# A two-layer hybrid decoder step on one core: the first step behind a norm goes set by set over both weight halves, with smaller first and last sets, a split sum of squares, and an earlier weight split

## The reference, cut to what matters

```python
for layer in range(DEPTH):                      # 2 layers
    mp = adaln(c_prompt, w_ada[layer], b_ada[layer])   # 6 vectors: shift, scale, gate, twice
    ms = adaln(c_sample, w_ada[layer], b_ada[layer])
    hp = modulate(yp, g_mix[layer], mp[0], mp[1])      # rms_norm(x, g) * (1 + scale) + shift
    hs = modulate(ys, g_mix[layer], ms[0], ms[1])
    ...                                          # layer 0: hp @ w_in_ab, conv and GLA mixers
    ...                                          # layer 1: hp @ w_in_cd, gMLP and attention
    yp = yp + mp[2][:, None, :] * (op @ w_out[layer])
    ys = ys + ms[2][:, None, :] * (os_ @ w_out[layer])
    yp = swiglu_sublayer(yp, mp[3], mp[4], mp[5], g_ffn[layer], w_ffn_gate[layer], ...)
    ys = swiglu_sublayer(ys, ms[3], ms[4], ms[5], g_ffn[layer], w_ffn_gate[layer], ...)
y_prompt = rms_norm(yp, g_final)
y_sample = rms_norm(ys, g_final)
```

## Time and profile before

| what | value |
|---|---|
| median of 3 executions | 2903.96 us (2903.19 to 2906.10) |
| the profiled execution's own time | 2900.26 us |
| its span | 2898.3 us |
| mean granted TensorE clock | 0.957 of full speed |
| PE busy (matmuls) | 2741.6 us, 95% of the span |
| DVE, ACT, POOL busy | 48%, 40%, 3% |
| the chain that ended last | PE 87%, DVE 4%, DMA 4%, ACT 3%, the rest 2% |

### The profile page before, as it was taken

The page is one execution under the profiler, slowest core; times in us unless marked ns, Lnnn a source line. Parts: engine busy times, 40 slices in busy tenths (PEclk is TensorE's granted clock), DMA queues, the critical chain, the costliest instruction groups (busy, mean ns, idle before and its releaser), DMA issues.

```text
span 2898.3 us, 47711 instructions
## 1 busy us (share of the span) xinstructions
PE 2741.6 (95%) x20153; PEld 2520.2 (87%) x20153; DVE 1402.5 (48%) x1845; ACT 1149.1 (40%) x1429; POOL 87.8 (3%) x116
## 2 busy tenths in 40 slices
PE   5899997989999999999999899798999999999998
PEld 1698875878888888898999799688999999999998
DVE  1599856343444333344444556435545444454444
ACT  2333254343344322334343446424444423444443
POOL 1000010000000000000000000101000000000000
PEclk7899986999999999999999999779999999999999
DMA  9667783766777688777634433224344344444443
GB/s 386 273 253 291 277 200 97 292 233 262 281 276 276 262 317 329 282 277 287 233 141 167 163 139 144 73 93 170 120 170 168 132 160 178 174 163 155 147 160 132
DMA packets 75774, 603.57 MB, mean 208 GB/s; under 512 B 21029, under 2 KB 22373, under 8 KB 24050
## 3 DMA queue, kind: packets, MB, share of 16 engines
q1 hardware_dynamic: 75634, 601.54, 56.2%
HBM read 592.01 MB, written 9.49 MB: 208 GB/s over the span
## 4 chain that ended last, share of the span: by engine, by line
PE 87%; DVE 4%; DMA 4%; ACT 3%; issue 1%; SPq 0%; POOL 0%; DVEq 0%; POOLq 0%; ACTq 0%
PE ps L654 26%; PE ps L656 25%; PE ps L655 25%; PE ps L784 5%; DMA pre_ring<-in_w_ada 3%; DMA aring<-in_w_ada 1%; DVE w_lo L1437 1%; ACT w_hi L1087 1%; PE ps L797 0%; DVE cacc L1532 0%; DVE act_lo L1635 0%; PE ps L769 0%; ACT tn L1250 0%; DVE tn L1616 0%; PE ps L1017 0%
## 5 line engine op out<-in xcount | busy, mean ns | idle before, releaser
L1437 DVE TENSOR_TENSOR w_lo<-raw,w_hi 128x2048 fp32r<-128x2048 f32 (+1 forms) x402 | 835.7, 2080 | 1112.6 <-ACT w_hi L1087 1112.4
L654 PE MATMUL ps<-act_hi,w_hi 128*128 128x288 f32 x4320 | 1294.3, 300 | 43.3 <-DVE act_lo L1635 31.4
L655 PE MATMUL ps<-act_hi,w_lo 128*128 128x288 f32 x4320 | 1279.0, 296 | 0.0
L656 PE MATMUL ps<-act_lo,w_hi 128*128 128x288 f32 x4320 | 1274.3, 295 | 0.0
L1087 ACT ACTIVATE w_hi<-raw 128x2048 fp32r<-128x2048 f32 (+1 forms) x402 | 699.3, 1741 | 1086.3 <-PE ps L656 1074.9
L654 PEld LDWEIGHTS ps<-act_hi,w_hi 128*128 128x128 f32 x4320 | 814.0, 188 | 104.4 <-issue 94.9
L656 PEld LDWEIGHTS ps<-act_lo,w_hi 128*128 128x128 f32 x4320 | 817.4, 189 | 0.0
L655 PEld LDWEIGHTS ps<-act_hi,w_lo 128*128 128x128 f32 x4320 | 815.4, 189 | 0.1
L654 PE MATMUL ps<-hid_hi,w_hi 128*128 128x288 f32 x1408 | 420.6, 299 | 8.6 <-DVE w_lo L1437 8.6
L655 PE MATMUL ps<-hid_hi,w_lo 128*128 128x288 f32 x1408 | 417.0, 296 | 0.0
L656 PE MATMUL ps<-hid_lo,w_hi 128*128 128x288 f32 x1408 | 415.5, 295 | 0.0
(11 more groups left out here) (271 smaller groups left out, 1429.9 us busy)
## 6 DMA issues: line engine op xcount, KB each, us to landing
aring<-in_w_ada SPq DMA_DIRECT2D x176, 1024.0 KB, 8.0
raw<-in_w_gu SPq DMA_DIRECT2D x88, 2048.0 KB, 8.1
raw<-in_w_dn SPq DMA_DIRECT2D x64, 1408.0 KB, 6.0
raw<-in_w_ab SPq DMA_DIRECT2D x20, 2048.0 KB, 8.1
raw<-in_w_out SPq DMA_DIRECT2D x16, 2048.0 KB, 8.2
raw<-in_w_cd SPq DMA_DIRECT2D x13, 2048.0 KB, 8.1
pre_ring<-in_w_ada SPq DMA_DIRECT2D x16, 1024.0 KB, 10.2
aring<-in_state_glaT SPq DMA_DIRECT2D x4, 1024.0 KB, 7.4
```

The lines of the kernel that those rows point to most:

```text
L654: pe.matmul(bank, w_hi[:, h, cols], hi[:, kt, :], start=begin, stop=False)
L655: pe.matmul(bank, w_lo[:, h, cols], hi[:, kt, :], start=False, stop=False)
L656: mm = pe.matmul(bank, w_hi[:, h, cols], lo[:, kt, :], start=False, stop=end)
L1437: dve.tensor_tensor(w_lo[:, h, 0:w], raw[:, par, h * w:(h + 1) * w], w_hi[:, h, 0:w].bitcast(F32), ALU.subtract).then_inc(split_done, 1)
```

## The change

The change has five parts.

1. **Restart.** The first step behind norms 1, 2 and 3 is done by a new function `restart` on PE: for each set of tiles it does half 0 and then half 1 of that set, into two PSUM banks, before it waits for the next set. An ada pair of that step now stands ahead of it.
2. **Sets.** For these norms the 16 tiles go in five sets of 2, 4, 4, 4 and 2 tiles, where there were four sets of 4.
3. **The splits around it.** Ahead of the norm, half 1 of the first step is split in two parts of 8 tiles: ACT does the first part ahead of the epilogue's squares and the second behind them; DVE does both behind its residual. `scales` moves from the norm's start to the step before it. Behind the restart, half 0 of the following step is split as 6 and 10 tiles: the first part may start when PE is through with half 0 of the second set (`part_done`), the second when half 0 of the whole restart is done; PE waits for the second part only ahead of tile 6.
4. **The last square.** For norms 1 to 4 POOL adds only 15 squares; PE multiplies the last square with the ones itself and accumulates.
5. **Ahead of `down`.** `then_wait` is no longer set for a step that stands ahead of a `down` segment, so half 1 of the first `down` step is split ahead of the last `gu` epilogue. (The segment `gu` that begins layer 1's feed-forward has its first body outside the loop now, since its first step is a restart.)

```diff
-    _s.peel = _s.bodies - 1 if _s.unrolled else int(_s.bodies == 2 or _s.opens or _s.kind == "out")
+    _s.peel = _s.bodies - 1 if _s.unrolled else int(_s.bodies == 2 or _s.opens or _s.kind == "out" or
+                                                    _s.kind == "gu" and _s.first == 0)
...
-        _a.then_wait = not isinstance(_b, Seg) or "down" in (_a.kind, _b.kind)
+        _a.then_wait = not isinstance(_b, Seg) or _a.kind == "down"
...
+PE_SQUARES = [39, 55, 79, 95]
+SETS = [(0, 2), (2, 6), (6, 10), (10, 14), (14, 16)]
+EARLY = 6
...
-                for k in range(n):
+                for k in range(n - (q + n - 1 in PE_SQUARES)):
...
-                pe.wait_ge(split_done, n * 2 + (h + 1))
+                in_parts = h == 0 and isinstance(n, int) and n - 1 in RESTARTS
+                if in_parts:
+                    pe.wait_ge(part_split, RESTARTS.index(n - 1) + 1)
+                else:
+                    pe.wait_ge(split_done, n * 2 + (h + 1))
...
+                    if in_parts and k == EARLY:
+                        pe.wait_ge(split_done, n * 2 + 1)
...
+            def restart(n, par):
+
+                pe.wait_ge(drained, n - 1)
+                for k0, k1 in SETS:
+                    pe.wait_ge(act_ready, sets[0] * KT + k1)
+                    for h in range(2):
+                        bank = ps[:, 2 * par + h, 0:T]
+                        if k0 == 0:
+                            pe.wait_ge(split_done, n * 2 + (h + 1))
+                        for kt in range(k0, k1):
+                            cols = slice(kt * P, (kt + 1) * P)
+                            pe.matmul(bank, w_hi[:, h, cols], act_hi[:, kt, :], start=(kt == 0), stop=False)
+                            pe.matmul(bank, w_lo[:, h, cols], act_hi[:, kt, :], start=False, stop=False)
+                            mm = pe.matmul(bank, w_hi[:, h, cols], act_lo[:, kt, :], start=False, stop=(kt == KT - 1))
+                        if k1 == EARLY and h == 0:
+                            mm.then_inc(part_done, 1)
+                        if k1 == KT:
+                            mm.then_inc(half_done, 1)
...
-                pe.matmul(ps[:, STAT_BANK, 0:T], ones[:], ssq[:], start=True, stop=True).then_inc(stat_ready, 1)
+                mm = pe.matmul(ps[:, STAT_BANK, 0:T], ones[:], ssq[:], start=True, stop=not split)
+                if split:
+                    pe.wait_ge(sq_ready, last + 1)
+                    mm = pe.matmul(ps[:, STAT_BANK, 0:T], ones[:], square_of(last), start=False, stop=True)
+                mm.then_inc(stat_ready, 1)
...
+                    if first and n in RESTARTS:
+                        if p is not None:
+                            ada_pair(p)
+                        restart(n, par)
+                        continue
...
+            def split_behind_restart(seg, n, par):
+
+                act.wait_ge(part_done, RESTARTS.index(n - 1) + 1)
+                high_part(seg, n, par, 0, 0, EARLY).then_inc(part_hi, 1)
+                act.wait_ge(half_done, n * 2 - 1)
+                high_part(seg, n, par, 0, EARLY, KT).then_inc(hi_done, 1)
...
+                    if nxt and end and seg.norm_next:
+                        act.wait_ge(half_done, n * 2 + 2)
+                        high_part(nxt, n + 1, 1 - par, 1, 0, CT).then_inc(first_hi, 1)
                     epilogue(seg, n, par, ls)
...
+                    if nxt and end and seg.norm_next:
+                        high_part(nxt, n + 1, 1 - par, 1, CT, KT).then_inc(hi_done, 1)
+                    elif nxt and hurry and not seg.mixed_next:
                         split(nxt, n + 1, 1 - par, 1)
...
-                scales(k, 0, KT)
                 if norm_base(k):
                     dve.wait_ge(act_ready, norm_base(k))
                 dve.wait_ge(rstd_ready, NORM_STATS[k])
-                for g in range(4):
+                for g in range(len(SETS)):
                     scaled(k, g)
                     samples(k, g)
                     if g:
                         lo(k, g - 1)
-                lo(k, 3)
+                lo(k, len(SETS) - 1)
```

More of the change, by code:

```diff
@@ L144, with sets_of, set_no, taken_by_pe @@
 SQUARES = [0, 16, 24, 40, 56, 64, 80, 96]
+PE_SQUARES = [39, 55, 79, 95]
 NORM_STATS = [1, 3, 4, 6, 7]
+SETS = [(0, 2), (2, 6), (6, 10), (10, 14), (14, 16)]
+EARLY = 6
 Y_PARTS = [slice(0, 2), slice(2, 4), slice(4, 8), slice(8, 12), slice(12, 14), slice(14, 16)]
 GLA_A = 4 * PRE + 2 * MIX_PAIRS
+def sets_of(k):
+    return SETS if k else [(4 * g, 4 * g + 4) for g in range(4)]
+def set_no(k, g):
+    return (4 + len(SETS) * (k - 1) if k else 0) + g
+def taken_by_pe(q):
+    return sum(q > last for last in PE_SQUARES)
 def lin(i, per, c):
@@ L312, in build @@
         amod_ready = sem("amod_ready")
+        part_done, part_hi, part_split, first_hi = (sem(name) for name in ("part_done", "part_hi", "part_split", "first_hi"))
         sel2_ready = sem("sel2_ready")
@@ L813, in stat @@
                 k = stats[0]
-                pe.wait_ge(sq_added, SQUARES[k + 1])
+                last = SQUARES[k + 1] - 1
+                split = last in PE_SQUARES
+                pe.wait_ge(sq_added, last + 1 - taken_by_pe(last + 1))
                 if k:
                     pe.wait_ge(rstd_ready, k)
-                pe.matmul(ps[:, STAT_BANK, 0:T], ones[:], ssq[:], start=True, stop=True).then_inc(stat_ready, 1)
+                mm = pe.matmul(ps[:, STAT_BANK, 0:T], ones[:], ssq[:], start=True, stop=not split)
[3 more added lines that the diff above has]
+                mm.then_inc(stat_ready, 1)
                 stats[0] += 1
@@ L1103, in stat_rstd, with wait_square @@
                 make_rstd(n).then_inc(rstd_ready, 1)
-            def wait_square(q):
+            def wait_square(q, skipped=0):
                 if not (isinstance(q, int) and q < 2):
-                    act.wait_ge(sq_added, q - 1)
+                    act.wait_ge(sq_added, q - 1 - skipped)
             def epilogue(seg, n, par, ls):
@@ L1204, in body @@
                         conv_affine()
-                    if nxt:
+                    if nxt and isinstance(n, int) and n in RESTARTS:
+                        split_behind_restart(nxt, n + 1, 1 - par)
+                    elif nxt:
                         split(nxt, n + 1, 1 - par, 0)
@@ L1231, in body @@
                         stat_rstd(CT * P)
-                    if nxt and hurry and not seg.mixed_next:
+                    if nxt and end and seg.norm_next:
+                        high_part(nxt, n + 1, 1 - par, 1, CT, KT).then_inc(hi_done, 1)
+                    elif nxt and hurry and not seg.mixed_next:
                         split(nxt, n + 1, 1 - par, 1)
@@ L1245, in norm_group @@
                 shift = layer * 96 + part * 48
-                act.wait_ge(tn_ready, 4 * k + g + 1)
-                act.wait_ge(amod_ready, 4 * k + g + 1)
-                for b in range(4):
-                    j = 4 * g + b
+                k0, k1 = sets_of(k)[g]
+                act.wait_ge(tn_ready, set_no(k, g) + 1)
+                act.wait_ge(amod_ready, 4 * k + (4 if k else g + 1))
+                for b in range(k1 - k0):
+                    j = k0 + b
                     ins = act.activation(tn[:, g % 2, b, 0:NP_TOK], tn[:, g % 2, b, 0:NP_TOK], ACT.Identity,
@@ L1252, in norm_group @@
                 L.link(ins)
-                act.wait_ge(tn_samples, 4 * k + g + 1)
-                act.activation(act_hi[:, 4 * g:4 * g + 4, :], tn[:, g % 2], ACT.Copy).then_inc(nhi_done, 1)
+                act.wait_ge(tn_samples, set_no(k, g) + 1)
+                act.activation(act_hi[:, k0:k1, :], tn[:, g % 2, 0:k1 - k0], ACT.Copy).then_inc(nhi_done, 1)
             def mix0(after):
@@ L1438, in split_lo, with low_part, split_lo_behind_restart @@
                                   ALU.subtract).then_inc(split_done, 1)
+            def low_part(seg, n, par, h, k0, k1):
+                at0 = h * KT * P
+                return dve.tensor_tensor(w_lo[:, h, k0 * P:k1 * P], raw[:, par, at0 + k0 * P:at0 + k1 * P],
+                                         w_hi[:, h, k0 * P:k1 * P].bitcast(F32), ALU.subtract)
+            def split_lo_behind_restart(seg, n, par):
+                dve.wait_ge(part_hi, RESTARTS.index(n - 1) + 1)
+                low_part(seg, n, par, 0, 0, EARLY).then_inc(part_split, 1)
+                dve.wait_ge(hi_done, n * 2 + 1)
+                low_part(seg, n, par, 0, EARLY, KT).then_inc(split_done, 1)
             def resid(seg, bank, j, b, first_inc, last_inc):
@@ L1563, in body @@
                     if nxt:
-                        split_lo(nxt, n + 1, 1 - par, 0)
+                        if isinstance(n, int) and n in RESTARTS:
+                            split_lo_behind_restart(nxt, n + 1, 1 - par)
+                        else:
+                            split_lo(nxt, n + 1, 1 - par, 0)
+                        if end and seg.norm_next:
+                            dve.wait_ge(ada_biased, PRE + (4 if seg.norm_next == 1 else 20))
```

(8 more changed lines are left out.)

46 lines of the change are left out of this document (29 added, 17 removed).

## The result

The changed kernel takes **2866.99 us** (2865.93 to 2871.32, 4 executions), the kernel before beside it 2904.97 (2903.19 to 2906.1, 4 executions): ratio 0.9873, 95% interval 0.9856 to 0.989, that is 38.0 us faster. Run again on another occasion it took 2867.59 against 2901.3, ratio 0.988 (0.9864 to 0.9895), 33.7 us.

The account below looks back on a forecast made before the run. PE, busy 95% of the span, was taken as the bound, so only its idle and half-clock time could be won. Terms of 6.7 + 4.6 + 4.6 + 1.0 + 1.8 + 0.3 + 1.0 + 7.8 = 27.8 us gave 2876.0 us, range 2870 to 2882.

Parts of the forecast that it names:

- The restart: First step behind norms 1 to 3: ends 19.1 us behind t0, winning 6.7, 4.6 and 4.6 us.
- t0: Start of DVE's first scaled set at a norm; the forecast counts the restart's times from it.
- the forecast's own case of PE waiting for sets: In the restart, if the clock never falls, PE waits for sets and the step ends at 18.7 us.
- S - t0: From t0 to ACT's start on half 1 of the step behind: 19.4 us, before 26.1, 24.0 and 24.0.
- a sign of being wrong: Behind a restart: granted clock of 0.50 over more than 5 us, among the signs that would show the forecast wrong.
- The rival by the Trainium skill: Clock stays at half through each restart, ending 28 us behind t0: 1 us won in all, 2903 us; chance 0.05.
- The tail of the restart: Splits of tiles 6 to 15 behind the restart end just in time: costed at nothing, bound 1 us per norm.
- The borders: From gu to down: the 2.60 us waits go away three times, 7.8 us; the first border's 0.75 as nothing.
- The time ahead of t0: Stat and scaling ahead of the first set: 1.0, 1.8 and 0.3 us won at norms 1 to 3; 1.0 at norm 4.
- SP's queue: Weight loads behind the restart: requested earlier, so the queue holds nothing up; no cost counted.
- More than forecast: Clock doesn't fall at some norm and the first border's 0.75 stays won: 32 us, 2872 or less; chance 0.07.

Follow-up runs that it names:

- e4: Changed kernel, but the restart takes half 0 through all five sets and then half 1: 2878.86 us, ratio 0.9925.
- e5: Changed kernel with the restart in four sets of 4 tiles and the first 8 tiles split early: 2872.06 us, ratio 0.9902.
- e7: Changed kernel, but half 0 of the step behind a restart is split in one piece again: 2881.71 us, ratio 0.9934.
- e1: Kernel before plus only the line that splits down's half 1 ahead of the last gu epilogue: 2884.1 us, ratio 0.9944.
- e2: Changed kernel without the line for the split ahead of down: 2883.17 us, ratio 0.9941.
- e10: e8, but DVE waits for POOL's last addition ahead of the low parts at norms 1 and 3: 2862.23 us, ratio 0.9864.
- e9: e8 with six sets of 1, 2, 3, 4, 4 and 2 tiles: 2864.99 us, ratio 0.9881.
- e8: Changed kernel with mix1's constants and cached keys and values loaded behind q's second weights: 2863.75 us, ratio 0.9867; again 2863.76, 0.9874.

## Why the prediction was right, and where its size was off

**The restart** held: first sets at 3.97 (forecast 4.05), the low parts of the next two sets 7.3 and 10.6 behind t0, as forecast, and 17.0 us won (15.9). The next step starts 18.8 behind t0, which is the forecast's own case of PE waiting for sets (18.7) and not the 19.1 taken. S - t0 at 19.37, 19.35 and 19.36 (forecast 19.4) agrees by luck: S now follows ACT's split of tiles 6 to 15 (1636.66 and 1.27 long at norm 2) and no longer the last matmul, and this makes up for the 0.3. The clock was at 2.4 GHz from the second set on in the profile shown, but clearly later in five of the 21 restarts counted above. In four of these it stayed at 0.50 for over 5 us, which the forecast named as a sign of being wrong; it cost 0.7 to 1.1 us each time. e4 and e5 show that both parts of the restart, the halves at each set and the small first set, carry the gain. The rival by the Trainium skill ("TensorE: Matmul & The Clock Gate", section "HAM oscillation — how this bites in real kernels"), a clock at half through the whole restart, didn't come true with these sets: at norms 2 and 3 PE waits 0.3 us at most for the second set and not for the later ones, and the clock was back 2.9 to 6.2 us behind its first matmul. DVE's rate was worked out from a subtraction and a multiplication; a subtraction of 576 elements takes 0.76 here, so nothing hangs on it.

**The tail of the restart** held: ACT takes 1.27 and DVE 1.49 for tiles 6 to 15, PE doesn't wait for tile 6, and e7 gives the price of the edit, 14.1 us.

**The borders** were mis-sized: "The 2.60 us go away three times: 7.8", and the first border's 0.75 as nothing. The two feed-forward stretches win 13.1, e1 alone 13.9 between the same places. The step that failed is the price of a stall: it was taken as its own length from the one border shown, the only one of the three in that profile behind which the clock didn't fall. At the others it costs 2.77 (start to start 2.90, less 0.133) and 1.6 behind it, 4.4. In layer 1 this adds up: two such borders are 8.7, and the stretch wins 8.76; e2, with the clock up behind one of the two, is 7.25 longer there than the changed kernel (2.77 + 4.4 = 7.2). In layer 0 the rest is the first border and the waits around its ada weights; which of the two isn't told apart here. That stretch takes 958.8 to 964.3 us in the eleven traces with the line and 966.2 to 968.8 in the three without, 6.1 apart on average, so the 4.30 of the result's profile is a low one.

**The time ahead of t0** held at norm 2 and at the end (2.05 and 1.10 for 1.8 and 1.0), and failed at norms 1 and 3 by 0.9 and 0.75 us. The step that failed is "POOL still adds one (0.87 us, half of 1.73)": the addition takes 1.71, because the changed order puts DVE's subtraction beside it. e10 removes that overlap and gets 0.95 to 0.99 back at norm 3. The Trainium skill says of it ("GPSIMD Engine Reference", section "1. Specifications") that GpSimd shares its SBUF interfaces with VectorE and contends with its instructions of two SBUF inputs. The subtraction has two, and the trace agrees: 0.79 alone, 1.71 beside it. At norm 1 PE's clock during the four products weighs as much: in four traces of this order (the changed kernel's two, e2, e9) they run at 1.2 GHz and t0 is 5.90 behind the last matmul, in five (e4, e5, e7, e8, e8_again) at 2.4 GHz and it is 4.85, which wins 1.16 where 1.0 was forecast.

**SP's queue** failed: "SP's queue holds nothing up" looked at the weights behind the restart and not at the eight loads that stand ahead of `q`'s second slot. They wait for norm 2 to be reported. In the kernel before, the load behind them was issued at 1653.82 and used at 1665.10, 11.3 us later; now it is issued at 1636.78 and would be used some 7 us later, so it lands 3.5 late, and 1.5 of that reach PE. e8 removes these 1.5.

In sum 27.8 + 5.3 (borders) - 1.5 (q) - 0.2 (restarts, time ahead of t0 and end together) = 31.4, which is what the profiles give without the opening. The medians give 33.7 and 38.0. Layer 0's average would add 1.8; the rest is within the interval (30.5 to 39.5 by the second ratio), and no row assigns it.

The rival "More than forecast" gave 32 us, near this, but for another reason: the clock did stay up at norm 1, and there PE waits 1.59 for the second set instead, so that the step ends at 18.8 as at the others. Two parts of the change, the earlier `scales` and the split in two parts ahead of the norm, were not run alone; their share isn't shown.
